# One half of K kept back and row transposes placed inside the bursts, in the opening of a fused two-block kernel

## What is computed

```python
c_act = jax.nn.silu(c)
for l in range(DEPTH):
    mod = c_act @ w_mod[l] + b_mod[l]                  # 2048 -> 6144
    shift, scale, gate = jnp.split(mod, 3, axis=-1)
    h = rmsnorm(x, norm_gain[l]) * (1.0 + scale[:, None, :]) + shift[:, None, :]
    proj = h @ w_in[l]                                 # 2048 -> 7504
...
    x = x + gate[:, None, :] * (y @ w_out[l])
```

## Time and profile before

| | |
|---|---|
| median of three runs | 1903.96 us (1903.75 to 1904.86) |
| profiled execution | 1904.12 us |
| its span in the trace | 1902.3 us |
| TensorE busy | 1848.3 us, 97% |
| VectorE busy | 1362.5 us, 72% |
| ScalarE busy | 985.9 us, 52% |
| moved by DMA | 424.27 MB, mean 223 GB/s |

### The profile page before, as it was taken

How to read it: one execution, slowest core, us unless ns; L and a number is a source line. 1 busy time by engine, 2 the same in 40 slices (tenths; PEclk the granted TensorE clock), 3 DMA queues, 4 the chain that set the end, 5 groups by cost and what they waited for, 6 DMA issues and landing times.

```text
span 1902.3 us, 23947 instructions
## 1 busy us (share of the span) xinstructions
PE 1848.3 (97%) x8992; PEld 1534.9 (81%) x8992; DVE 1362.5 (72%) x1964; ACT 985.9 (52%) x1344; POOL 202.0 (11%) x256
## 2 busy tenths in 40 slices
PE   4989999999999999999999999999999999999997
PEld 3768788888887877888888888888888888888886
DVE  7888999988996778856765544488775465665555
ACT  6554455446446445544654644476664445444464
POOL 0000002100000000210000000044341020031001
PEclk9879999999999999999999999999999999999999
DMA  9998978965995986744365555554445555557552
GB/s 338 340 354 297 329 253 289 314 223 172 319 324 188 351 292 232 243 155 156 124 221 193 183 190 189 195 177 151 159 154 162 193 194 183 178 182 259 177 189 99
DMA packets 211825, 424.27 MB, mean 223 GB/s; under 512 B 7681, under 2 KB 12557, under 8 KB 210317
## 3 DMA queue, kind: packets, MB, share of 16 engines
q1 hardware_dynamic: 209516, 413.08, 64.2%
q10 hardware_dynamic: 2208, 9.85, 1.3%
HBM read 418.69 MB, written 4.21 MB: 222 GB/s over the span
## 4 chain that ended last, share of the span: by engine, by line
PE 93%; ACT 2%; DVE 2%; issue 1%; DMA 0%; ACTq 0%; DVEq 0%; POOLq 0%; POOL 0%
PE acc L663 27%; PE acc L665 27%; PE acc L664 27%; PE sps L1042 1%; PE sps L771 1%; PE acc L830 1%; PE tps L704 1%; PE acc L832 1%; PE acc L831 1%; PE tps L746 1%; PE tps L793 1%; ACT w_hi L1210 1%; DVE proj L1904 0%; DVE w_lo L1807 0%; PE sps L963 0%
## 5 line engine op out<-in xcount | busy, mean ns | idle before, releaser
L1807 DVE TENSOR_TENSOR w_lo<-raw,w_hi 128x1024 fp32r<-128x1024 f32 (+1 forms) x580 | 721.2, 1250 | 464.2 <-ACT w_hi L1210 461.8
L1210 ACT ACTIVATE w_hi<-raw 128x1024 fp32r<-128x1024 f32 (+1 forms) x580 | 606.8, 1051 | 773.8 <-PE acc L665 694.8
L663 PE MATMUL acc<-w_hi,ht_hi 128*128 128x512 f32 (+1 forms) x2304 | 910.9, 395 | 2.4 <-DVE ht_lo L1867 1.9
L665 PE MATMUL acc<-w_hi,ht_lo 128*128 128x512 f32 (+1 forms) x2304 | 894.3, 388 | 0.0
L664 PE MATMUL acc<-w_lo,ht_hi 128*128 128x512 f32 (+1 forms) x2304 | 892.5, 387 | 0.0
L663 PEld LDWEIGHTS acc<-w_hi,ht_hi 128*128 128x128 f32 x2304 | 433.3, 188 | 90.1 <-DVE ht_lo L1867 3.1
L665 PEld LDWEIGHTS acc<-w_hi,ht_lo 128*128 128x128 f32 x2304 | 432.6, 188 | 90.2
L664 PEld LDWEIGHTS acc<-w_lo,ht_hi 128*128 128x128 f32 x2304 | 433.7, 188 | 83.3
L1931 DVE SCALAR_TENSOR_TENSOR scr<-raw,vcol,scr 128x512 f32<-128x512 f32 x154 | 111.0, 762 | 4.6 <-DMA raw<-in_w_mod 0.2
L2021 DVE SCALAR_TENSOR_TENSOR scr<-raw,vcol,scr 128x1024 f32<-128x1024 f32 x56 | 68.3, 1279 | 2.6 <-DMA raw<-in_w_mod 2.4
L1931 DVE SCALAR_TENSOR_TENSOR proj<-raw,vcol,proj 128x512 f32<-128x512 f32 x70 | 52.3, 789 | 1.9
(11 more groups left out here) (299 smaller groups left out, 1488.9 us busy)
## 6 DMA issues: line engine op xcount, KB each, us to landing
raw<-in_w_in SPq DMA_DIRECT2D x208, 1024.0 KB, 5.1
raw<-in_w_mod SPq DMA_DIRECT2D x64, 1024.0 KB, 6.0
raw<-in_w_mod SPq DMA_DIRECT2D x64, 512.0 KB, 6.1
raw<-in_w_out SPq DMA_DIRECT2D x32, 1024.0 KB, 5.1
raw<-in_w_o SPq DMA_DIRECT2D x16, 1024.0 KB, 5.1
raw<-in_w_ple_gate SPq DMA_DIRECT2D x16, 1024.0 KB, 5.1
raw<-in_w_b_out SPq DMA_DIRECT2D x8, 1024.0 KB, 5.1
raw<-in_w_a_out SPq DMA_DIRECT2D x8, 1024.0 KB, 5.0
```

The lines of the kernel that those rows point to most:

```text
L663: pe.matmul(o, hi_m, w_hi[:, slot, u, 0:width], start=start, stop=False)
L665: mm = pe.matmul(o, lo_m, w_hi[:, slot, u, 0:width], start=False, stop=stop)
L1210: act.activation(w_hi[:, x % SPL, :, 0:width], raw[:, j, 2 * (x % halves):2 * (x % halves) + 2, 0:width], ACT.Copy).then_inc(hi_ready, 1)
L1807: dve.tensor_tensor(w_lo[:, x % SPL, :, 0:width], raw[:, j, 2 * (x % halves):2 * (x % halves) + 2, 0:width], w_hi[:, x % SPL, :, 0:width]. ...
```

## The change

The round is put together anew, on all three engines.

- The fourth half of a round, (g, h) = (1, 1), is kept back. TensorE uses it only behind the next round's `pair_sums` (in the last round directly behind the third half); ScalarE rounds it behind `formed_tiles`, and VectorE takes its low part last.
- The transposes of the rows for the next round (`turn_rows`) stand behind the first and the second half of a round, each followed by a step; ScalarE copies them (`turned_rows`) behind `scaled_rows`.
- VectorE multiplies the first block (j = 0) of the next round ahead of the tiles' low parts. It counts that in a semaphore of its own, `early_read`; `first_read` adds the two counts to `raw_read` behind the fourth `w_lo`.
- `row_root` is put behind the third step instead of the sixth.
- `STEPS` is now 7 + 6 + 6 + 5. In each round those behind the third half stand in a row.
- `PIECES`: a piece is moved from half 7 of chunk 14 to half 1 of chunk 13, in layer 0. Its sum is made and read where it was.

In the diff, `modulate` holds the products of one block as the loop of before did, `turn_rows` the four transposes of a row pair, `quarter_half` the twelve matmuls of a half.

```diff
@@ PIECES and STEPS
-           12: (7,), 13: (3, 7), 14: (7,), 15: (1, 3), 16: FULL, 17: FULL, 18: (1, 3)},
+           12: (7,), 13: (1, 3, 7), 15: (1, 3), 16: FULL, 17: FULL, 18: (1, 3)},
-STEPS = [(6, 1, 4), (1, 1, 4), (1, 1, 4), (1, 0, 0)]
+STEPS = [(7, 6), (0, 6), (0, 5), (0, 0)]
@@ SUM_AT
-                        if k == 14:
-                            SUM_AT[n], TAKE_AT[n] = (l, k + 1, 7), (l, k + 2, 3)
+                        if k == 13:
+                            SUM_AT[n], TAKE_AT[n] = (l, k + 2, 7), (l, k + 3, 3)
@@ TensorE
-            n = 0
-            for i, (a, c, d) in enumerate(STEPS):
...
+            def turn_rows(k):
+                pe.wait_ge(xs_ready, M * (k // 4 + 1))
+                if k:
+                    pe.wait_ge(xt_ready, k // 2)
...
+                tr.then_inc(xt_turned, 1)
+            def quarter_half(i, g, h):
+                if g == 0:
+                    t_lo.skip(2)
+                    pe.wait_ge(turn_lo, t_lo.ahead(2))
+                pe.wait_ge(raw_read, 8 + 20 * i + 16 + 2 * g + h + 1)
...
+                mm.then_inc(split_used, 1)
+            pe.wait_ge(acc_taken, taken.next(2))
+            steps(0, 6)
+            turn_rows(0)
+            turn_rows(2)
+            n = 6
+            for i, (a, d) in enumerate(STEPS):
+                pair_sums()
                 if i:
-                    steps(n, a)
+                    quarter_half(i - 1, 1, 1)
+                else:
+                    steps(6, 1)
+                    n = 7
+                quarter_half(i, 0, 0)
+                if i < 3:
+                    turn_rows(4 * i + 4)
+                    steps(n, 1)
+                quarter_half(i, 0, 1)
+                if i < 3:
+                    turn_rows(4 * i + 6)
+                    steps(n + 1, 1)
+                quarter_half(i, 1, 0)
+                if i < 3:
+                    steps(n + 2, d - 2)
+                n += d
+            quarter_half(3, 1, 1)
@@ ScalarE
-            n = 0
-            for i, (a, c, d) in enumerate(STEPS):
-                if i == 0:
-                    steps(0, a)
-                    row_root()
-                    scaled_rows(0)
-                for k in (4 * i, 4 * i + 2):
-                    turned_rows(k)
-                if i:
-                    steps(n, a)
...
-                steps(n + a, c)
-                formed_tiles(i)
-                if i < 3:
-                    scaled_rows(i + 1)
-                steps(n + a + c, d)
-                n += a + c + d
+            steps(0, 3)
+            row_root()
+            steps(3, 3)
+            scaled_rows(0)
+            turned_rows(0)
+            turned_rows(2)
+            n = 7
+            for i, (a, d) in enumerate(STEPS):
+                for g, h in ((0, 0), (0, 1), (1, 0)):
+                    quarter_rounded(i, g, h)
+                if i == 0:
+                    steps(6, 1)
+                formed_tiles(i)
+                quarter_rounded(i, 1, 1)
+                if i < 3:
+                    scaled_rows(i + 1)
+                    turned_rows(4 * i + 4)
+                    steps(n, 1)
+                    turned_rows(4 * i + 6)
+                    steps(n + 1, d - 1)
+                n += d
@@ VectorE
+            def modulate(i, j):
...
+            def first_read(i):
+                dve.wait_ge(early_read, 2 * i + 2)
+                dve.wait_ge(raw_read, own.ahead(0))
+                dve.sem_inc(raw_read, 2)
+                own.skip(2)
+            m_free.skip(8)
+            modulate(0, 0)
             for i in range(4):
-                dve.wait_ge(mod_summed, m_free.next(2))
-                for j in range(8):
...
+                first_read(i)
+                for j in range(1, 8):
+                    modulate(i, j)
                     if i == 0 and j == 3:
                         row_sum()
                     if i == 0 and j == 5:
                         row_inverse()
...
...
+                for g, h in ((0, 0), (0, 1), (1, 0)):
+                    quarter_low(i, g, h)
+                columns(i)
+                if i < 3:
+                    modulate(i + 1, 0)
+                tiles_low(4 * i)
+                tiles_low(4 * i + 2)
+                quarter_low(i, 1, 1)
```

More of the change, by code:

```diff
@@ L338, in build @@
         tiles_formed = sem("tiles_formed")
+        early_read = sem("early_read")
         keys_spread = sem("keys_spread")
@@ L795, in pair_sums @@
                 mm.then_inc(mod_summed, 2)
-            n = 0
-            for i, (a, c, d) in enumerate(STEPS):
-                if i == 0:
-                    steps(0, a)
-                for k in (4 * i, 4 * i + 2):
[L802 to L809, removed]
-                if i:
-                    steps(n, a)
-                pair_sums()
-                steps(n + a, c)
[L814 to L836, removed]
@@ new lines, in turn_rows @@
+            def turn_rows(k):
+                pe.wait_ge(xs_ready, M * (k // 4 + 1))
+                if k:
+                    pe.wait_ge(xt_ready, k // 2)
+                for e in range(2):
+                    for m in range(M):
+                        o = e * S + m * P
+                        tr = pe.transpose(tps[:, 0, o:o + P], xs[:, m, (k + e) * P:(k + e + 1) * P], ident)
+                tr.then_inc(xt_turned, 1)
[4 more added lines that the diff above has]
+                pe.wait_ge(raw_read, 8 + 20 * i + 16 + 2 * g + h + 1)
+                for u in range(2):
+                    kt = 4 * i + 2 * h + u
+                    for m in range(M):
+                        hi_m, lo_m = (t[:, kt, m * P:(m + 1) * P] for t in (ht_hi, ht_lo))
+                        o = acc[:, g, m, :]
+                        pe.matmul(o, hi_m, w_hi[:, 2 * g + h, u, :], start=kt == 0, stop=False)
+                        pe.matmul(o, hi_m, w_lo[:, 2 * g + h, u, :], start=False, stop=False)
+                        mm = pe.matmul(o, lo_m, w_hi[:, 2 * g + h, u, :], start=False, stop=kt == KT - 1)
+                mm.then_inc(split_used, 1)
@@ L837, in _ @@
+            quarter_half(3, 1, 1)
+            lo.skip(80)
             pe.wait_ge(bias_ready, 6)
@@ L2008, in columns @@
                                          v1("norm_gain", 4 * i, 4), ALU.add, ALU.mult).then_inc(columns_ready, 1)
-            for i in range(4):
-                dve.wait_ge(mod_summed, m_free.next(2))
-                for j in range(8):
[L2013 to L2024, removed]
+            def modulate(i, j):
+                slot = (10 * i + j) % RAW
+                dve.wait_ge(raw_landed[slot], m_land[slot].next(32))
+                for u in range(2):
+                    kt, src, to = 2 * j + u, raw[:, slot, 2 * u:2 * u + 2, :], macc[:, :, u, :]
+                    if j == 0:
+                        dve.tensor_scalar(to, src, v2("c", kt), None, ALU.mult).then_inc(early_read, 1)
+                    else:
+                        dve.wait_ge(raw_read, own.ahead(-1))
+                        dve.scalar_tensor_tensor(to, src, v2("c", kt), to, ALU.mult, ALU.add).then_inc(raw_read, 1)
+                        own.skip(1)
@@ new lines, in first_read, with quarter_low @@
+            def first_read(i):
[3 more added lines that the diff above has]
+                own.skip(2)
+            def quarter_low(i, g, h):
+                dve.wait_ge(hi_ready, hi.next())
+                dve.tensor_tensor(w_lo[:, 2 * g + h, :, :], raw[:, (10 * i + 8 + g) % RAW, 2 * h:2 * h + 2, :],
+                                  w_hi[:, 2 * g + h, :, :].bitcast(F32), ALU.subtract).then_inc(raw_read, 1)
+                own.skip(1)
@@ L2031, in _ @@
                 for g in range(2):
[L2032 to L2045, removed]
+                    m_land[(10 * i + 8 + g) % RAW].skip(16)
+                for g, h in ((0, 0), (0, 1), (1, 0)):
[6 more added lines that the diff above has]
+                quarter_low(i, 1, 1)
             results.skip(16)
```

22 lines of the change are left out of this document (11 added, 11 removed).

## The result

The changed kernel takes 1915.87 us (median of 4 runs, 1914.51 to 1916.75) against 1904.28 (4 runs, 1903.75 to 1904.86) for the kernel before: 1.0060 of its time, interval 1.0043 to 1.0078. That is 11.6 us slower. Forecast were 1905.0 and a range up to 1911, so the prediction was wrong in its size and outside its range. Of its rivals it is the second that came nearest: TensorE was the bound and its clock fell, though mainly in the halves behind the gaps and not in the steps that this rival names, and it cost 10.9 us over the forecast instead of 6. The profiled execution of after took 1916.75 us, with a span of 1914.9 us against 1902.3.

What follows compares the result with a forecast made beforehand. In the opening, TensorE, VectorE and the DMA engines stand within some 3 us of each other per round. Opening +3.1 us and moved piece -2.0 sum to +1.1 on 1904.0, about 1905.0; range 1896.5 to 1911.

Steps and rivals of the forecast that it cites:

- T: End of VectorE's addition at L2030 (mod_ready) in an opening round; forecast at about 39, 73, 104 and 136.
- S: Start of the second block (j = 1) of the next round's products at L2021; before, at 51.62.
- Root sooner: Opening: VectorE's 3.33 us root wait goes, first T at 39.0, first S at 51.3 against 51.62: -0.3 us.
- S to T, the price of the kept half: Opening: blocks 13 and 14 both ordered at S, so products wait for loads: 20.9 us (20.2 to 21.6) against 18.9.
- the fixed 4.3 us: Opening loads: fixed part of the 12.5 us from order to landing of three blocks, beside 2.71 us each.
- T to S: Opening: VectorE's 1.22 us wait for the first w_hi goes; 10.7 us (10.0 to 11.3) against 11.3.
- The end: Opening's last burst: ends at T + 19.9 against T + 21.5, -1.6 us (bounds -2.5 and -0.5).
- rival 2: Opening: TensorE becomes the bound at the lower clock, steps about 2.0 us in place of 1.5; 1911 us; chance 0.20.
- its other case: Opening: the clock never rises, a round takes some 39 us, the kernel is over 20 us slower; 2%.
- Its point of decision: Opening: rival 2 decides as soon as TensorE isn't done with its steps when VectorE's addition ends.
- my sign for it: Opening: for rival 2, sums start over 1 us behind T with VectorE's products not waiting for loads.
- The moved piece: Chunks 14 and 13: stall removed -3.9 us, retention wait +1.9, together -2.0 (bounds -3.9 and 0).

Runs made afterwards that it cites:

- after, gaps filled: The changed kernel with 36 matmuls of 512 columns added where TensorE waits in the two gaps of a burst, order unchanged: 1904.46 us, ratio 1.0003.
- both: ahead, none kept: The changed kernel with steps ahead of row turns and the fourth half in its burst, not kept back: 1899.01 us, ratio 0.9971.
- and a step ahead of every burst: The version with steps ahead of turns and no half kept, plus one step per round moved to where TensorE waits for tiles: 1894.48 us, ratio 0.9944.
- the exchange: The changed kernel with the step put ahead of the row turns in both gaps, on TensorE and ScalarE, half still kept back: 1902.93 us, ratio 0.9993.

## Why the prediction was wrong

Read from VectorE's timelines, in us (T and S as in the prediction; "end" is from the last T to chunk 2's first matmul):

| kernel | S to T | T to S | end | chunk 2 at |
|---|---|---|---|---|
| before | 18.9, 19.0, 18.5 | 11.3, 11.4 | 21.5 | 152.4 |
| as predicted | 21.3, 20.9, 20.9 | 10.7 | 19.9 | 155.5 |
| after | 20.1, 20.0, 20.0 | 15.0, 15.5 | 24.1 | 166.4 |
| after, steps ahead of turns | 20.1, 20.1, 21.0 | 10.6, 10.6 | 20.0 | 154.1 |
| after, gaps filled | 20.0, 20.0, 20.7 | 11.1, 11.5 | 19.6 | 154.7 |
| after, no half kept | 18.1, 18.4, 18.2 | 20.9, 16.0 | 29.0 | 170.9 |
| both: ahead, none kept | 18.6, 18.1, 18.1 | 11.5, 12.3 | 22.0 | 150.7 |
| and a step ahead of every burst | 18.2, 18.6, 18.3 | 9.6, 9.1 | 21.4 | 145.4 |

**Root sooner: right.** T came at 39.1, forecast 39.0, and S at 51.67 in place of 51.3.

**S to T, the price of the kept half: right in kind, over-sized.** Two orders together at S, the thin stretch of loads, the wait on the third block and 0.20 to 0.28 us on each later one are all there. But the third block's waits were 0.64, 0.58 and 0.45 us, not 1 or more; in the second round it landed 5.5 us behind S, where one block and the fixed 4.3 us give 7.0, and the fifth block landed at S + 16.4, where I took 17.2 and had 16.5 as the lower bound. The mis-sized term is the 4.3 us: it wasn't all fixed. In the stretch that it was read from, 52.0 to 64.2 us of the kernel before, the DMA engines moved 318 GB/s in the mean, which is 3.9 MB and not the 3.1 MB of three blocks. The rest was, as far as the trace tells, of loads ordered later, and is worth 1.9 us at 385 GB/s, an estimate. The 1.4 us that I had allowed for two orders at once is of the right size, but no row gives it. So +3.6 us in three rounds stand against +6.4 forecast. That the half kept back is what costs this is shown by taking it out: 18.1 us.

**T to S: the step that failed.** I took 10.7 us, bounds 10.0 and 11.3; it was 15.0 and 15.5, which is 9.1 us over the sum in two rounds. The bounds rested on the sums being ready at T + 3.7. That needs TensorE and ScalarE to be done with their steps at T. In after the steps held TensorE until 75.39, T + 3.6, and the kept half behind the sums, at 5.3 us, then held the fourth slot of w_hi, as the upper bound had it. So each part of that bound is shifted by the same delay. In the next round the sums start 5.2 us behind T.

**The end: the same step.** Forecast T + 19.9, measured T + 24.1: the sums start at 146.42, 4.2 us behind T. With the exchange it is 20.0 us, as worked out.

**Where the delay comes from: the clock, left out of the forecast's own sum.** For the first round I had TensorE done near S + 22 and called that 0.4 us behind T. By my own T, S + 20.9, it is 1.1, so the 0.4 was too small already. Measured were S + 23.7 in after and S + 20.7 with filled gaps. For the later rounds I wrote "near T, with about 1 us to spare", and for that took every half but the first at 2.8 us. The gap's time I had in the sum. What I had not, in the forecast or in rival 2, is that a gap can make the half behind it slow. Rival 2 has the clock fall among the steps behind the third half, where each step loses 0.5 us, and prices it at 2 us a round; its other case is a clock that never rises. In fact it rose and fell within a burst, and 10.6 us of halves were added. Its point of decision, TensorE not done with its steps when VectorE's addition ends, was the right one. Of my sign for it only half was met: the sums start 3.6 us behind T, but VectorE's products wait for loads as well. I gave a single chance in fifty to a clock that never rises, since dense halves had always raised it; the halves in question were no longer dense. The row to weigh was in the same group: 1.1 us between halves, with one step, is all that it shows, and I carried it over to gaps of 3.5 to 4.6 us.

The Trainium skill, "TensorE: Matmul & The Clock Gate", section "HAM oscillation — how this bites in real kernels", describes a kernel whose idle gaps send the clock down again, so that the next tile starts slow. The runs here agree that a gap can do this, at a price of 11.4 us between after and the filled gaps. But these gaps are not idle: in the first, TensorE waits 1.63 us of 3.8 and does small operations in the rest. I had cited that page's first part for what it would do for the kept half and not asked what it would do in the gaps.

**The moved piece: right.** -2.0 forecast, -1.4 behind the opening in after, -2.4 between the medians of the run with it alone.

**The sum.** +3.1 forecast for the opening; S 0.35 over, S to T 2.8 under, T to S 9.1 over, the end 4.2 over: +14.0, as measured. With the clock kept up the kernel takes 1902.9 or 1904.5 us, close to the 1905.0 that I had priced. The prediction was of a kernel whose clock stays up; that 1904.5 comes so near is in part luck: with filled gaps the stretches from S to T are 2.4 us shorter in all than forecast, and those from T to S 1.2 us longer.

What stays open: why the clock holds in the second gap when the first is short, and in the second burst of the version without the half kept back, where neither is. The granted clock shows that it does, not why.

## What to carry to other kernels

When small operations are moved into a dense burst, count what TensorE waits for in each new gap and price the work behind it at both clocks; a sum that holds only at the upper one needs its own rival at the lower. In a gap that two engines share, put first the operation whose input is already there, and the one that must fetch a reply last. Where one engine already waits for another at a hand-over (here VectorE 1.22 us for ScalarE), what is saved on the waiting side (the next pair begun sooner) only lengthens the wait. It is the other side that has to come sooner; spreading the steps did that, and took 4.5 us off the version with the exchange and no kept half. And a part that costs waits may also give slack to another engine: without the half kept back the gaps cost 20.2 us (1919.2 against 1899.0), with it 13.0.

## What was not expected of the hardware

Waits of 1.27 and 0.36 us in a gap of 4.0 us, the rest of which is 4 transposes and 10 small matmuls, went with a granted clock of 0.50 for the whole half behind it (98.83 to 104.10); six matmuls more in such gaps, 1.4 us of work, kept it at 1.00. Gaps with the same two waits also stood without a fall, in two other versions. Adding 36 matmuls made the kernel 11.4 us faster. A load of 1 MiB that was ordered together with a second one landed 5.5 us behind S, 1.5 us sooner than I had worked out from three loads of the kernel before, ordered 2.4 us apart.
